# Two sets of semaphores in turn, and one barrier instead of two between the stages of a hybrid transformer step

## The reference

```python
def layer(x, c, q_pos, past, P, l):
    S0, shift0, ckv0, kr0, k0, v0 = past
    ...
    mod = jax.nn.silu(c.astype(jnp.float32)) @ P['w_ada'][l] + P['b_ada'][l]
    shift, scale, gate = jnp.split(mod[:, None, :], 3, axis=-1)
    h = rms_norm(x, P['norm_g'][l]) * (1.0 + scale) + shift
    proj = h @ P['w_in'][l]
    pr, zA, cq, ckv, kr, zB, sq, sk, sv, zC, gates = _split(proj, IN_SIZES)
    yA, S1, shift1 = rwkv7_branch(pr, shift0, S0, P, l)
    yB, ckv1, kr1 = mla_branch(cq, ckv, kr, ckv0, kr0, q_pos, k_pos, P, l)
    yC, k1, v1 = sb_branch(sq, sk, sv, k0, v0, q_pos, k_pos)
    gA, gB, gC = jnp.split(jax.nn.sigmoid(gates), 3, axis=-1)
    merged = (gA * ((yA * jax.nn.silu(zA)) @ P['w_br_rwkv'][l])
              + gB * ((yB * jax.nn.silu(zB)) @ P['w_br_mla'][l])
              + gC * ((yC * jax.nn.silu(zC)) @ P['w_br_sb'][l]))
    x = x + gate * (merged @ P['w_out'][l])
    return x, (S1, shift1, ckv1, kr1, k1, v1)
```

## Time and profile before

| | |
|---|---|
| median of three timed runs | 4704.79 us (4702.94 to 4711.39) |
| the profiled execution | 4707.36 us |
| its span, first to last instruction | 4705.5 us |
| mean granted TensorE clock | 0.967 of full speed |
| TensorE busy | 4334.4 us, 92% |
| VectorE, ScalarE, GpSimd busy | 48%, 35%, 17% |
| DMA | 280.77 MB, mean 60 GB/s |

### The profile page before, as it was taken

One profiled execution on the slowest core, in us unless ns is written; L12 is line 12 of the kernel. 1 busy time (PEld: TensorE's weight loads), 2 busy tenths in 40 slices (PEclk: granted clock), 3 DMA queues, 4 the chain that ended last, 5 costly groups with the idle time before them and its releaser, 6 DMA issues. The chain is left out here.

```text
span 4705.5 us, 74875 instructions
## 1 busy us (share of the span) xinstructions
PE 4334.4 (92%) x29488; PEld 3017.3 (64%) x29488; DVE 2280.0 (48%) x4684; ACT 1643.2 (35%) x3886; POOL 814.2 (17%) x980
## 2 busy tenths in 40 slices
PE   7999998989989989999979999989888999899999
PEld 3666665667666667777436666655666566677774
DVE  2556664345524453534425665633455244535344
ACT  4333433445523442211043334333555234421220
POOL 0011010000010015544300110000000100245443
PEclk9999998999999999999989999999999999999999
DMA  5110012010021112222241210120100211123222
GB/s 195 23 35 13 28 25 87 14 36 14 12 87 56 53 65 92 95 102 76 85 192 23 35 15 26 25 88 17 31 16 11 87 58 57 70 88 111 89 72 84
DMA packets 150655, 280.77 MB, mean 60 GB/s; under 512 B 51546, under 2 KB 77402, under 8 KB 145059
## 3 DMA queue, kind: packets, MB, share of 16 engines
q1 hardware_dynamic: 150306, 275.99, 18.3%
HBM read 230.96 MB, written 42.62 MB: 58 GB/s over the span
## 5 line engine op out<-in xcount | busy, mean ns | idle before, releaser
L1054 PE MATMUL banks<-hT,w_piece 128*128 128x384 f32 x1536 | 545.2, 496 | 4.4 <-ACT raw L1159 4.1
L1054 PEld LDWEIGHTS banks<-hT,w_piece 128*128 128x128 f32 x1536 | 279.4, 193 | 171.6 <-issue 11.8
L2233 PE MATMUL banks<-hT,w_piece 128*128 128x384 f32 x1056 | 354.1, 489 | 1.5 <-ACT sb_gate_raw L2343 1.5
L2233 PEld LDWEIGHTS banks<-hT,w_piece 128*128 128x128 f32 x1056 | 196.1, 190 | 141.4 <-issue 16.6
L1999 DVE SCALAR_TENSOR_TENSOR keysT<-banks,gains,rstd 64x128 f32<-64x128 f32 (+1 forms) x272 | 112.1, 412 | 252.9 <-ACT rstd L1913 250.4
L2689 DVE TENSOR_TENSOR gate_quarters<-gate_kept,banks 128x288 f32<-128x288 f32 x144 | 65.4, 454 | 298.4 <-PE banks L2552 293.4
L2640 ACT ACTIVATE gate_kept<-banks 128x288 f32<-128x288 f32 x144 | 59.0, 410 | 431.9 <-PE banks L2552 431.9
L2689 DVE TENSOR_TENSOR branch_quarters<-branch_kept,banks 128x288 f32<-128x288 f32 x144 | 65.4, 454 | 265.0 <-PE banks L2552 264.7
L2405 DVE TENSOR_TENSOR_SCAN left<-pass,zero 128x384 f32<-128x384 f32 (+7 forms) x144 | 190.5, 1323 | 5.0
L2402 DVE TENSOR_TENSOR pass<-pass,constants 128x128 f32<-128x128 f32 x128 | 40.8, 319 | 312.8 <-ACT take L2354 310.2
L1015 POOL TENSOR_TENSOR state_decayed<-state,decay_of_chunk 128x128 f32<-128x128 f32 x120 | 85.9, 716 | 547.4 <-DVE state L1288 547.4
(11 more groups left out here) (425 smaller groups left out, 9801.8 us busy)
## 6 DMA issues: line engine op xcount, KB each, us to landing
w_piece<-in_w_cols SPq DMA_DIRECT2D x66, 512.0 KB, 4.4
w_ada<-in_w_ada SPq DMA_DIRECT2D x24, 1024.0 KB, 9.6
w_gate_ahead<-in_w_cols SPq DMA_DIRECT2D x48, 512.0 KB, 4.3
w_branch<-in_w_br SPq DMA_DIRECT2D x96, 256.0 KB, 2.9
w_gate<-in_w_cols SPq DMA_DIRECT2D x48, 512.0 KB, 4.3
y_branch<-y_gated SPq DMA_DIRECT2D x12, 1152.0 KB, 8.0
sb_cached_keysT<-in_sbkT SPq DMA_DIRECT2D x8, 1024.0 KB, 7.6
sb_cached_values<-in_sbv SPq DMA_DIRECT2D x8, 1024.0 KB, 5.1
```

Source lines behind the costliest of these rows:

```text
L1054: last = mm(dst, w[0 if kind in ("k", "v") else 1][:, k, :], hT[:, k, c], start=(k == 0), stop=(k == KD - 1))
L2233: last = mm(ps[:, bank[n], 0:TG], w_of[wn][:, k, :], hT[:, k, TG * g:TG * g + TG], start=(k == 0), stop=(k == KD - 1))
```

## The change

`Stages.stage` no longer gives each stage the semaphore numbers of the one before. It has two ranges of numbers, 48 apart (`room`), and takes them in turn: stage 1 and every odd one the first range, every even one the second. Leaving a stage, POOL still clears that stage's range behind the block's barrier, but the barrier behind the clear is gone: the other engines go on to the next stage, whose semaphores are of the other range, while POOL clears. The range just cleared is taken again two stages on, with the next block's barrier, in which POOL takes part, between.

```diff
     def __init__(self, nc):
-        self.nc, self.k, self.first = nc, 0, None
+        self.nc, self.k, self.first, self.room = nc, 0, None, 48
...
         for n in names:
-            sems.append(nc.alloc_semaphore(f"{n}_{self.k}", **({} if self.first is None else {"num": self.first + len(sems)})))
-            self.first = sems[0].num
+            if self.first is None:
+                sems.append(nc.alloc_semaphore(f"{n}_{self.k}"))
+                self.first = sems[0].num
+            else:
+                sems.append(nc.alloc_semaphore(f"{n}_{self.k}", num=self.first + self.room * ((self.k + 1) % 2) + len(sems)))
         lo, hi = sems[0].num, sems[-1].num
-        assert hi - lo == len(sems) - 1
+        assert hi - lo == len(sems) - 1 < self.room
...
         nc.gpsimd.sem_clear(range(lo, hi + 1))
-        nc.all_engine_barrier()
         for s in sems:
             nc.release_semaphore(s)
```

## The result

The changed kernel took 4680.6 us (median of 5 executions, 4666.3 to 4686.3) against 4706.5 us before (5, 4702.9 to 4712.8): a ratio of 0.9936, 95% interval 0.9918 to 0.9954. In a second comparison, with 6 and 23 executions, it was 4683.3 against 4704.1 us, 0.9954 (0.9941 to 0.9966). So the change gives 22 to 30 us, where 13.4 were forecast for the barriers. The first median lies 2.4 us under the stated range, the second 0.3 us inside its lower end.

What follows compares the result with a forecast made beforehand. TensorE, busy 92% of the span, was taken as the bound. Over 29 boundaries, 7.8 us of barriers plus 5.8 us of clears, less 0.2 us, gave 13.4 us off 4704.79 us: 4691 us, range 4683 to 4699.

Steps and rivals of the forecast that it cites:

- The price of a boundary: At 29 stage boundaries, barrier 0.27 us (7.8 us) plus wait for POOL's clear 0.20 us (5.8 us): 13.6 us.
- The clear beside the stage at no cost: POOL's clear runs beside TensorE's first matmuls of a stage, price 0; 0.2 us comes back at the very end.
- So the whole of each stage slides forward: At each boundary one event releases everything, so stages start earlier and the path takes the whole 13.4 us.
- The rival with the clock: Shorter TensorE pauses before solve stages keep the clock up; six gain about 1.7 us each: 4681 us, chance 0.13.
- Scattered stores: Rival: ACT's waits before line 1153 for out_shift_s stores lengthen, up to 5.9 us each; four make 4715 us, chance 0.03.
- The sign named for it: Fused stages of 86 us and more where 80 is usual would show the stores rival.
- The draws: Stores and clock vary between executions, moving a median of a few runs by some 4 us; timed runs within 8.5 us.
- the three parts of "faster": Chance of under 4695.4 us: forecast 0.64, clock 0.13, a quarter of the clear rival's 0.11; given as 0.81.

Runs made afterwards that it cites:

- before, and twice more with its boundaries: Kernel before; repeated unedited, ratio 1.0002; and the changed kernel's two semaphore ranges with the second barrier put back, ratio 1.0002.
- four products at the head: Kernel before plus four identity products heading TensorE's list in each of 8 fused stages with a recurrence: 4706.2 us, ratio 0.9996.
- barrier left out at the other 21: Changed kernel with the second barrier kept at the 8 solve-to-fused boundaries, left out at the other 21: 4688.7 us, ratio 0.9968.
- left out at these 8 only: Changed kernel with the second barrier left out only at the 8 solve-to-fused boundaries, kept at 21: 4694.9 us, ratio 0.9979.
- kept at work, both kernels: Identity products added behind TensorE's last matmul of several stages: on the kernel before 4679.6 us (0.9933), on the changed kernel 4666.0 us (0.9911).
- the fastest version: Changed kernel plus identity products at the ends of solve, fused, latent attention and latent pairs stages: 4666.0 us, ratio 0.9911.

## Why the prediction was wrong

- **The price of a boundary** was right as a sum: over the 29 places the trace of before has 13.9 us from first to second release, the prediction 13.6, and the waits of the stages' first matmuls fell nearly by the amounts given. Its two parts were not: a barrier alone takes 0.33 us and not 0.27, and taking only the clear off the path saves 3.9 us and not 5.8. For this change, which takes both, it makes no difference.
- **The clear beside the stage at no cost** was right: the first hand-over of a solve stage takes 0.84 us with and without the clear beside it, at the same clock.
- **"So the whole of each stage slides forward"** was the step that failed. The stages did not only slide, they got shorter: by 8 to 17 us after the two ratios (21.6 and 30.1 us less 13.4), 27.7 us in the first trace, through TensorE's clock. The sum had this term at nothing; the prediction saw it only as a rival, with a chance of 0.13.
- **The rival with the clock** had the mechanism, but the wrong places, so that its 4681 us met the 4680.6 us was luck. It looked for solve stages at 1.00; in the first trace they stayed at 0.94 to 0.95. The gain came in the fused stages' starts, where TensorE's pause was short already (1.04 us), and, in part perhaps by chance, inside latent pairs, where no boundary is near. The earlier trace rows showed the clock of the solve stages alone, not of the others.
- **Scattered stores.** No part: the wait that was 53.2 us is 54.5 us after. The sign named for it did come up, a first fused stage of 89.0 us in the second trace, but traces with the boundaries of before have 86.9 and 89.0 us there as well.
- **The draws** were under-rated: executions of the kernel before spread over 36 us, not 8.5.
- **A slip in the chances:** the three parts of "faster" (0.64, 0.13 and a quarter of 0.11) make 0.80, not 0.81.

The clock's part can be sized from the mean clock of each execution: time at 1.2 GHz is twice the missing share of the span (a clock of 0.967 in 4705.5 us means 311 us; the third decimal is worth 9 us). Over 82 executions of the kernel before, each microsecond more at 1.2 GHz goes with 0.36 us more time, with a correlation of 0.89. Their mean is 4705.1 us with 300 us at 1.2 GHz; that of the changed kernel's eleven is 4680.8 us with 266 us. The 35 us less at 1.2 GHz would be worth 12.5 us by that slope, and with the 13.7 us of boundaries that left the path (the 13.9 us less the last clear) it makes 26 us, where 24 were measured. The same can be seen without a slope: at the same mean clock of 0.971, six executions of before have a mean of 4695.1 us and four of the changed kernel 4683.0, 12 us apart, close to the price of the barriers alone. The slope is an estimate and not a pure price of the clock, because an execution in which TensorE waits longer for something else is both longer and lower in its clock.

The Trainium skill (TensorE: Matmul & The Clock Gate, "What's actually happening") holds that the clock's activity window runs free of the kernel. By that rule where a pause falls matters and not only its length. The runs agree in two ways: executions of one kernel spread from 4685.9 to 4722.2 us, and the same pause of 1.04 us is followed by 1.2 GHz in some kernels and not in others. They also show what the rule alone does not let one expect: with the boundaries of before, the same six stages started at 1.2 GHz in each of three executions.

What stays open is how the 8 to 17 us divide between shorter pauses and better alignment. Here are the six fused stages in all traces (a start counts as slow when the clock of its first 3.4 us is under 0.75):

| kernel | TensorE idle in front, us | slow starts |
|---|---|---|
| before, and twice more with its boundaries | 1.04 | 18 of 18 |
| four products at the head | 1.04 | 4 of 6 |
| barrier left out at the other 21 | 1.04 | 3 of 6 |
| both barriers, the clear behind | 0.95 | 3 of 6 |
| left out at these 8 only | 0.62 | 4 of 6 |
| changed, two traces | 0.62 | 1 of 12 |
| one barrier more | 1.37 | 5 of 6 |
| two more | 1.70 | 5 of 6 |
| kept at work, both kernels | 0.82 and 0.40 | 0 of 12 |

Long pauses have more slow starts on the whole, but the same pause comes with very different counts, so its length alone is ruled out. No experiment changed the alignment of the whole kernel by a fixed amount with the pauses kept, so alignment is the likely rest and not shown. Of most kernels there is one trace, so counts that differ by one or two tell nothing. Nor is the latent pairs stage explained: it lasts 375 to 385 us in the traces with both barriers and 376 to 383 us in those without, and it is long in both layers of the fastest version.

## What to carry to other kernels

A pause in which TensorE stands still costs itself and, where TensorE is the bound, it can cost a share of what follows at 1.2 GHz; so when a wait at a stage's boundary is priced, the granted clock of the first microseconds behind every boundary belongs in the sum, for all kinds of stages and from more than one trace. A price found as a difference inside a longer wait, as the barrier's 0.27 us beside a clear, need not hold when the other part is gone. Work that TensorE can do in the shadow of others (even useless products, if they fit into the pause at the lower clock) was worth as much here as the change itself, 27 to 31 us, and both together gave 40 us. Two sets of semaphores in turn make the second barrier needless, and the numbers themselves cost nothing (ratio 1.0002).

## What the runs showed of the hardware

- An all-engine barrier directly behind another takes 0.33 us from release to release (median of 29 in three kernels). With a clear of 71 to 244 ns between the two it is 0.34 to 0.52 us in most places, so the clear adds less than its length.
- Clearing a range of semaphores takes 71 ns for 6 and 244 ns for 39 of them. Beside a running stage it did not delay the first hand-over from TensorE to VectorE (0.84 us with and without, at a clock of 1.00).
- Two executions of one program had the same six stage starts at 1.2 GHz, and 19 of their 28 stages had the same length to 0.1 us. Four products more per round, 8.5 us of work at least, changed two of the six starts and cost no time that can be told (ratio 0.9996).
- Longer is not always slower: 29 barriers more, 10.3 us by themselves, changed the time by 1 to 3 us; 58 more, 19.8 us, by 24 to 27 us.
